# A hybrid decoder trunk with expert retrieval: GpSimd gathers the row of v ahead of the row of u in each slot

## The chip, the cores and the metric

The kernel runs on one core of a Trainium2 chip. The metric is the device time in microseconds, from one launch to its end. Three runs of the kernel before gave 3232.33, 3233.42 and 3233.64 us; the median is 3233.42 us. Lower is better.

## The reference

The reference is a decoder trunk of two layers on 512 tokens of width 1024, in float32. Each layer normalises x, runs three kinds of causal mixer side by side (a state-space group, a stick-breaking attention group and a sparse attention group), adds their projected output to x, and then adds a retrieval step:

```python
def peer_ffn(h, w_q, sub_keys, u_tab, v_tab):
    ...
        eidx = i1 * N_KEYS + i2
        g = jax.nn.softmax(cv, axis=-1)
        u = u_tab[eidx]
        v = v_tab[eidx]
        a = jax.nn.gelu(jnp.einsum('thkd,td->thk', u, xb).astype(jnp.float32), approximate=False)
        return jnp.einsum('thk,thkd->td', (g * a).astype(v.dtype), v)
```

For every token, 8 heads choose 16 experts each out of 16384. That is 128 experts per token, each with one row of 1024 numbers in the table u and one in the table v. The row of u is multiplied with the token (a dot product, then gelu and a gate weight), and the row of v is added to x with that weight. The change touches nothing but the order in which these rows are fetched.

## The kernel before, in words

The 512 tokens are four blocks of 128, one token to a partition. Two blocks make a step, so two layers make four steps (n = 0 to 3). A step has 256 **slots**: slot s stands for one expert of each of the 128 tokens of a block, 128 slots to a block, 16 to a head. In all there are 1024 slots (`GATHERS`), and each needs two gathers, one of u and one of v, of 128 rows of 4 KB (524,288 bytes).

All engines run one loop over s. The v side trails by `LAG` = 20 slots: in the pass for s the row of u belongs to slot s and the row of v to slot t = s - 20, since the weight of a head is known only when its 16 dot products are done. The last 20 passes have a v gather only.

- **GpSimd** (`pool_program`) issues both gathers, u at L1477 and v at L1490. The u rows land in a ring of 8 buffers, and so do the v rows. The gather of u for s waits until VectorE has used buffer s - 8 (`u_used`), at the start of a head also until the indices (`idx`) are there. The gather of v for t waits until t - 8 has been used: by TensorE (`v_used`) or by VectorE (`v_used_vector`). GpSimd takes its instructions in the order written, so a gather that waits holds all behind it.
- **VectorE** (`vector_program`) waits for u of slot s and forms the dot product (L1416). Where the slot t is its own (`BY_VECTOR`), it then waits for v of t and adds the weighted row to X (L1434). Every 16 slots it multiplies gelu and gate into the weights (L1424). At the end of a block it adds the sum that TensorE formed (L1439). Behind that come the pieces of the trunk and of the routing that are due at this slot.
- **TensorE** (`tensor_program`) takes the other slots: a matrix product of a diagonal of weights with the v rows, summed up in `acc` (L754). Before the first one of a block it waits for the sum of the block ahead (`x_done`). Then it does the trunk pieces due at this slot.
- **ScalarE** makes gelu (L1024) and the diagonals (L1032), and **SyncE** streams the weights of the trunk and writes the output.

VectorE takes one slot in 16 while no trunk work runs beside, otherwise every odd slot, and in the last step one in 4. The trunk of step n + 1 runs beside the gathers of step n, from its slot 90 on; the routing of a step (which finds the indices) runs into its own first 86 slots. In step 3 there is no trunk left to run beside.

Of the kernel before, what the change touches and what calls it, by code (L numbers as in the profile page):

```python
# [17 lines left out]
PEER_H, TOPK, KEYS = 8, 16, 128  # L18
# [18 lines left out]
PER_STEP = 2 * SLOTS  # L37
GATHERS = STEPS * PER_STEP
U_RING, V_RING, DIAG_RING = 8, 8, 5
# [182 lines left out]
def trunk(nc, x_dram, const_dram, param_dram, w_dram, u_dram, v_dram, out_dram):  # L222
# [4 lines left out]
    with ctx:  # L227
        def sb(name, shape, dt=fp32):
            return ctx.enter_context(nc.sbuf_tensor(name, shape, dt))
# [19 lines left out]
        u_rows, v_rows = sb("u_rows", [P, U_RING, D]), sb("v_rows", [P, V_RING, D])  # L249
        diag = sb("diag", [P, DIAG_RING, P])  # L250
        dots, gel, wgt = (sb(n, [P, 2, SLOTS]) for n in ("dots", "gel", "wgt"))
        idx = sb("idx", [P, 2, PER_STEP], u32)
# [77 lines left out]
        def sig(name):  # L330
            if name not in sems:
                sems[name] = ctx.enter_context(nc.semaphore(name))
            return sems[name]
# [36 lines left out]
        def nth(n, name, k):  # L370

            return n * PER[name] + k
# [54 lines left out]
        def before(v):  # L427

            return v - VECTOR_SUMS[v], VECTOR_SUMS[v]

        def phases_after(slot):

            return int((SLOT_OF <= slot).sum())
# [1009 lines left out]
        def pool_tracks(pool, n, chain):  # L1443
            l, p = divmod(n, PAIRS)
            heads = lambda t: t.rearrange("p (h d) -> p h d", d=HD)

            def all_():
                yield "n1b"
                if n == 0:
                    pool.wait_ge(sig("consts_in"), 16)  # L1450
                    made(G.memset(kcvcT[:], 0.0), "cache_zero")
                if p:
                    made(G.tensor_copy(xin[:, :, 0:TAPS - 1], tail[:]), "carry")
                else:
                    made(G.memset(xin[:, :, 0:TAPS - 1], 0.0), "carry")
                if p == 0:
                    yield "xt0"
                    wait_freed(pool, f"{n}.f7")
                    G.tensor_copy(tail[:], xin[:, :, PAIR:PAIR + TAPS - 1]).then_inc(sig("tail"), 1)
                    pool.wait_ge(sig("tail"), n // 2 + 1)  # L1460

            return [all_()]

        def pool_program(pool):
            chain = InOrder(pool, "pool_chain")
            run = Phases(lambda n: pool_tracks(pool, n, chain))
            run.upto(phases_after(-1))
            for s in range(GATHERS + LAG):
                n = s // PER_STEP
                if s < GATHERS:  # L1470
                    head = s % PER_STEP // TOPK
                    if s % TOPK == 0 and head <= PEER_H:
                        pool.wait_ge(sig("idx"), nth(n, "idx", 2 * head + 1 if head < PEER_H else 2 * PEER_H))
                    if s >= U_RING:
                        pool.wait_ge(sig("u_used"), s - U_RING + 1)
                    at_s = s % PER_STEP
                    pool.indirect_dma_start(  # L1477
                        out=u_rows[:, s % U_RING, :], out_offset=None, in_=u_dram,
                        in_offset=bass.IndirectOffsetOnAxis(ap=idx[:, n % 2, at_s:at_s + 1], axis=0),
                    ).then_inc(sig(f"u_in{s % U_RING}"), 16)  # L1480
                t = s - LAG
                if t >= 0:
                    if t >= V_RING:
                        old = t - V_RING
                        if BY_VECTOR[old]:
                            pool.wait_ge(sig("v_used_vector"), before(old)[1] + 1)
                        else:
                            pool.wait_ge(sig("v_used"), before(old)[0] + 1)
                    at_t = t % PER_STEP
                    pool.indirect_dma_start(  # L1490
                        out=v_rows[:, t % V_RING, :], out_offset=None, in_=v_dram,
                        in_offset=bass.IndirectOffsetOnAxis(ap=idx[:, t // PER_STEP % 2, at_t:at_t + 1], axis=0),
                    ).then_inc(sig(f"v_in{t % V_RING}"), 16)
                run.upto(phases_after(s - POOL_LAG))


# [29 lines left out]
        with nc.Block() as block:  # L1526
            @block.tensor
            def _(pe):
                tensor_program(pe)

            @block.scalar
            def _(act):
                scalar_program(act)

            @block.vector
            def _(dve):
                vector_program(dve)

            @block.gpsimd
            def _(pool):  # L1540
                pool_program(pool)

            @block.sync
            def _(sy):
                sync_program(sy)
# [18 lines left out]
```

## Time and profile before

| quantity | value |
|---|---|
| median of three runs | 3233.42 us |
| the profiled execution: its own time | 3229.1 us |
| its span | 3227.3 us |
| TensorE busy with matrix products | 2555.5 us (79%) |
| VectorE busy | 2429.2 us (75%) |
| GpSimd busy | 2115.9 us (66%) |
| ScalarE busy | 799.3 us (25%) |
| moved by the DMA engines | 1187.51 MB, mean 368 GB/s |
| of it by the gathers' queue | 1073.87 MB |

The profile comes from one execution, whose own time is 4.3 us under the median. The share of an engine is a mean over stretches that differ: in the first 300 us no gather can run yet, later the DMA engines, VectorE or TensorE set the pace in turn. In the rows of a timeline the first number is the start, the second the duration, and the brackets hold the idle time of the engine in front of the instruction and what ended it; "issue" means that it waited for nothing that the profile shows. The waits are given as engine and line, what was waited for, microseconds in total, times, longest.

### The profile page before, as it was taken

The page shows a single profiled execution, that of the slowest core. Times are in us where ns is not written, and L with a number is a line of the kernel's source. Part 1 is how long each engine was busy: PE and PEld are TensorE (multiplying, and loading weights), DVE is VectorE, ACT ScalarE, POOL GpSimd, SP SyncE. Part 2 cuts the span into 40 slices and gives each one's busy share as a digit, 9 for nine tenths or more (in the row PEclk, how much of TensorE's full clock was granted, in tenths as well). Part 3 has the DMA queues.
Part 4 walks back from the last instruction along what each step waited for, and adds up shares of the span by engine and source line. Part 5 has one row for each costly group of instructions (what it writes and reads, how often), then busy time and mean ns, then how long its engine had stood idle before and what let it go on. Part 6 is the DMA issues. An engine that isn't in the chain of part 4 may idle for free. (4 is left out here: it accounts for less than half of the span.)

```text
span 3227.3 us, 30187 instructions
## 1 busy us (share of the span) xinstructions
PE 2555.5 (79%) x8860; PEld 1512.6 (47%) x8860; DVE 2429.2 (75%) x5632; ACT 799.3 (25%) x1853; POOL 2115.9 (66%) x2059
## 2 busy tenths in 40 slices
PE   8877677898897686888788687899898587656667
PEld 7666433665464332665455342566566342222222
DVE  2324997768878997768878998758877999666664
ACT  2521222234321122223421122233431122111111
POOL 0001677657777777757776777766777777777775
PEclk9859799999898899898899799999899899998889
DMA  5104899999999999999999999999999999999999
GB/s 191 55 21 160 345 409 409 412 406 372 383 379 411 366 402 410 411 411 394 397 392 410 390 404 409 410 412 388 386 376 411 393 385 409 409 409 410 409 409 354
DMA packets 311313, 1187.51 MB, mean 368 GB/s; under 512 B 34544, under 2 KB 34544, under 8 KB 298352
## 3 DMA queue, kind: packets, MB, share of 16 engines
q0 software_dynamic: 294912, 1073.87, 84.7%
q1 hardware_dynamic: 16240, 111.72, 8.7%
q8 instruction: 73, 1.20, 0.1%
q14 instruction: 88, 0.72, 0.1%
HBM read 1183.36 MB, written 2.10 MB: 367 GB/s over the span
## 5 line engine op out<-in xcount | busy, mean ns | idle before, releaser
L754 PE MATMUL acc<-v_rows,diag 128*128 128x512 f32 x2728 | 1431.5, 659 | 485.7 <-DMA v_rows<-expert_v,idx 391.1
L1416 DVE CUSTOM_DVE_ANT_0 u_rows<-u_rows,h 128x1024 f32<-128x1024 f32 x1024 | 1231.4, 1216 | 398.4 <-DMA u_rows<-expert_u,idx 396.4
L1477 POOL DMA_INDIRECT u_rows<-expert_u,idx x1024 | 1057.0, 1032 | 625.6 <-DVE idx L1381 269.0
L1490 POOL DMA_INDIRECT v_rows<-expert_v,idx x1024 | 1057.2, 1032 | 425.6 <-issue 261.1
L754 PEld LDWEIGHTS acc<-v_rows,diag 128*128 128x128 f32 x2728 | 523.3, 207 | 1202.2 <-issue 985.4
L1434 DVE SCALAR_TENSOR_TENSOR X<-v_rows,wgt,X 128x1024 f32<-128x1024 f32 x342 | 439.2, 1284 | 43.5 <-DMA v_rows<-expert_v,idx 37.9
L1032 ACT ACTIVATE diag<-consts,wgt 128x128 f32<-128x128 f32 x682 | 255.1, 395 | 746.9 <-PE acc L754 567.9
L465 PE MATMUL bank<-HT,w_ring 128*128 128x256 f32 x1792 | 412.6, 386 | 2.2 <-DVE HT L1040 2.2
L465 PEld LDWEIGHTS bank<-HT,w_ring 128*128 128x128 f32 x1792 | 350.0, 196 | 93.3 <-issue 46.1
L474 PE MATMUL bank<-w_ring,HT 128*128 128x256 f32 (+1 forms) x1280 | 278.7, 375 | 2.6 <-ACT arena L765 2.6
L765 ACT ACTIVATE arena<-bank 128x256 f32<-128x256 f32 (+4 forms) x304 | 112.7, 382 | 664.5 <-PE bank L465 253.8
L474 PEld LDWEIGHTS bank<-w_ring,HT 128*128 128x128 f32 x1280 | 239.3, 193 | 56.3 <-issue 25.1
L1040 DVE TENSOR_TENSOR arena<-arena 128x256 f32<-128x256 f32 (+3 forms) x238 | 102.8, 435 | 4.7 <-ACT arena L765 3.5
L1024 ACT ACTIVATE gel<-dots 128x16 f32<-128x16 f32 x64 | 13.8, 216 | 332.1 <-DVE dots L1416 331.9
L686 PE MATMUL bank<-nkT,arena 64*128 64x128 f32 (+3 forms) x128 | 61.9, 571 | 29.9 <-ACT arena L961 27.2
L1416 DVE DVE_READ_ACCUMULATOR2_ANT dots<- 128x1 f32 x1024 | 85.0, 83 | 0.0
L734 PE MATMUL bank<-params,arena 128*128 128x128 f32 x256 | 43.0, 293 | 52.7 <-ACT arena L765 52.7
L456 PE MATMUL bank<-dg,X 128*128 128x128 f32 x256 | 42.9, 337 | 38.5 <-ACT dg L765 35.2
L1238 DVE TENSOR_REDUCE sm_mx<-bank 128x1 f32<-128x128 f32 (+3 forms) x64 | 31.3, 489 | 56.0 <-PE bank L687 56.0
L1290 DVE MAX8 arena<-arena 128x8 f32<-128x128 f32 (+1 forms) x192 | 52.9, 328 | 25.3 <-ACT arena L765 23.1
L734 PEld LDWEIGHTS bank<-params,arena 128*128 128x128 f32 x256 | 40.1, 203 | 63.3 <-ACT arena L765 56.8
L961 ACT ACTIVATE arena<-bank,sm_nm 128x128 f32<-128x128 f32 (+3 forms) x64 | 33.6, 526 | 128.7 <-DVE sm_nm L1239 50.0
(185 smaller groups left out, 1990.6 us busy)
## 6 DMA issues: line engine op xcount, KB each, us to landing
w_ring<-weights SPq DMA_DIRECT2D x100, 1024.0 KB, 8.0
u_rows<-expert_u,idx POOLq DMA_INDIRECT x1024, 11.0
v_rows<-expert_v,idx POOLq DMA_INDIRECT x1024, 11.2
X<-in_x SPq DMA_DIRECT2D x2, 1024.0 KB, 6.6
out<-X SPq DMA_DIRECT2D x4, 512.0 KB, 6.6
n2w_wide<-parameters SPq DMA_DIRECT2D x2, 512.0 KB, 8.4
params<-parameters SPq DMA_DIRECT2D x2, 412.0 KB, 7.6
consts<-constants SPq DMA_DIRECT2D x1, 749.5 KB, 6.4
```

What stands on the lines that cost most here:

```text
L465: last = T.matmul(out[:, 0:PAIR], cols(i)[:, k, m % 2 * P:(m % 2 + 1) * P], HT[:, k, :], start=(k == 0), stop=(k == KT - 1))
L474: last = T.matmul(out[:, 0:width], HT[:, k, blk[b]], cols(i)[:, k, 0:width], start=(k == 0), stop=(k == KT - 1))
L686: T.matmul(out[:, 0:width], nqT[base:base + 64, h // 2, blk[b]], nkT[base:base + 64, br, 0:width], start=True, stop=False)
L734: last = T.matmul(out[:, blk[b]], qT[m % 2][:, blk[b]], param("keys")[:, m % 2 * P:(m % 2 + 1) * P], start=True, stop=True)
L754: last = T.matmul(acc[:, at_h], diag[:, i % DIAG_RING], v_rows[:, t % V_RING, at_h], start=(at_t == 0), stop=(t == max(q for q in range(t ...
L765: return S.activation(dst, src, ACT.Copy, **k)
L1032: made(S.activation(diag[:, i % DIAG_RING], ident, ACT.Copy, scale=wgt[:, b % 2, at_t:at_t + 1]), "diag")
L1040: return V.tensor_tensor(out, in0, in1, op)
L1416: made(V.tensor_tensor_reduce(out=rows_u, in0=rows_u, in1=h2[:], scale=1.0, scalar=0.0, op0=ALU.mult, op1=ALU.add, accum_out=dots[:, b % 2 ...
L1434: made(V.scalar_tensor_tensor(Xb, v_rows[:, t % V_RING, :], wgt[:, b % 2, at_t:at_t + 1], Xb, ALU.mult, ALU.add), "v_used_vector")
L1477: pool.indirect_dma_start(out=u_rows[:, s % U_RING, :], out_offset=None, in_=u_dram, in_offset=bass.IndirectOffsetOnAxis(ap=idx[:, n % 2, ...
L1490: pool.indirect_dma_start(out=v_rows[:, t % V_RING, :], out_offset=None, in_=v_dram, in_offset=bass.IndirectOffsetOnAxis(ap=idx[:, t // PE ...
```

## The change

In the pass for s, GpSimd issued u of slot s and behind it v of slot s - 20. Now it issues v of slot s - 20 first, and u of slot s behind it. The waits stand with their gathers and move with them. The other engines' programs are as before.

```diff
--- before.py
+++ after.py
@@ -1467,17 +1467,6 @@
             run.upto(phases_after(-1))
             for s in range(GATHERS + LAG):
                 n = s // PER_STEP
-                if s < GATHERS:
-                    head = s % PER_STEP // TOPK
-                    if s % TOPK == 0 and head <= PEER_H:
-                        pool.wait_ge(sig("idx"), nth(n, "idx", 2 * head + 1 if head < PEER_H else 2 * PEER_H))
-                    if s >= U_RING:
-                        pool.wait_ge(sig("u_used"), s - U_RING + 1)
-                    at_s = s % PER_STEP
-                    pool.indirect_dma_start(
-                        out=u_rows[:, s % U_RING, :], out_offset=None, in_=u_dram,
-                        in_offset=bass.IndirectOffsetOnAxis(ap=idx[:, n % 2, at_s:at_s + 1], axis=0),
-                    ).then_inc(sig(f"u_in{s % U_RING}"), 16)
                 t = s - LAG
                 if t >= 0:
                     if t >= V_RING:
@@ -1491,6 +1480,17 @@
                         out=v_rows[:, t % V_RING, :], out_offset=None, in_=v_dram,
                         in_offset=bass.IndirectOffsetOnAxis(ap=idx[:, t // PER_STEP % 2, at_t:at_t + 1], axis=0),
                     ).then_inc(sig(f"v_in{t % V_RING}"), 16)
+                if s < GATHERS:
+                    head = s % PER_STEP // TOPK
+                    if s % TOPK == 0 and head <= PEER_H:
+                        pool.wait_ge(sig("idx"), nth(n, "idx", 2 * head + 1 if head < PEER_H else 2 * PEER_H))
+                    if s >= U_RING:
+                        pool.wait_ge(sig("u_used"), s - U_RING + 1)
+                    at_s = s % PER_STEP
+                    pool.indirect_dma_start(
+                        out=u_rows[:, s % U_RING, :], out_offset=None, in_=u_dram,
+                        in_offset=bass.IndirectOffsetOnAxis(ap=idx[:, n % 2, at_s:at_s + 1], axis=0),
+                    ).then_inc(sig(f"u_in{s % U_RING}"), 16)
                 run.upto(phases_after(s - POOL_LAG))
```

The line numbers move: the gather of v is L1479 in the changed kernel, that of u L1490.

On GpSimd, the place where the v gathers begin. Each row names line, target and source, and the semaphores waited for. Before:

```order
L1477 DMA u_rows<-expert_u,idx 128x1024 [waits u_used,idx]
L1477 DMA u_rows<-expert_u,idx 128x1024 [waits u_used] x4
L1490 DMA v_rows<-expert_v,idx 128x1024
L1477 DMA u_rows<-expert_u,idx 128x1024 [waits u_used]
L1490 DMA v_rows<-expert_v,idx 128x1024
L1477 DMA u_rows<-expert_u,idx 128x1024 [waits u_used]
```

And now:

```order
L1490 DMA u_rows<-expert_u,idx 128x1024 [waits u_used,idx]
L1490 DMA u_rows<-expert_u,idx 128x1024 [waits u_used] x3
L1479 DMA v_rows<-expert_v,idx 128x1024
L1490 DMA u_rows<-expert_u,idx 128x1024 [waits u_used]
L1479 DMA v_rows<-expert_v,idx 128x1024
L1490 DMA u_rows<-expert_u,idx 128x1024 [waits u_used]
```

The first v gather now stands ahead of u for slot 20 instead of behind it; from there on both orders alternate.

On GpSimd, the end of the program, from the last u gathers on. Before:

```order
L1477 DMA u_rows<-expert_u,idx 128x1024 [waits u_used]
L1490 DMA v_rows<-expert_v,idx 128x1024 [waits v_used]
L1477 DMA u_rows<-expert_u,idx 128x1024 [waits u_used]
L1490 DMA v_rows<-expert_v,idx 128x1024 [waits v_used_vector]
L1490 DMA v_rows<-expert_v,idx 128x1024 [waits v_used] x3
L1490 DMA v_rows<-expert_v,idx 128x1024 [waits v_used_vector]
```

And now:

```order
L1479 DMA v_rows<-expert_v,idx 128x1024 [waits v_used]
L1490 DMA u_rows<-expert_u,idx 128x1024 [waits u_used]
L1479 DMA v_rows<-expert_v,idx 128x1024 [waits v_used_vector]
L1490 DMA u_rows<-expert_u,idx 128x1024 [waits u_used]
L1479 DMA v_rows<-expert_v,idx 128x1024 [waits v_used] x3
L1479 DMA v_rows<-expert_v,idx 128x1024 [waits v_used_vector]
```

The last u gather (slot 1023) changed places with v of slot 1003, which waits for VectorE's use of slot 995. The v gathers from slot 1004 on are the same gathers at the same places of the sequence.

## Rows read from the trace of the kernel before

**Rows 1.** The page's slices: 40 equal parts, what the DMA engines moved in each, GB/s.

```profile
GB/s 191 55 21 160 345 409 409 412 406 372 383 379 411 366 402 410 411 411 394 397 392 410 390 404 409 410 412 388 386 376 411 393 385 409 409 409 410 409 409 354
```

**Rows 2.** Stretches: us; busy PE, PEld, DVE, ACT, POOL; clock, DMA share, GB/s.

```profile
720.00:960.00 240.00, 213.00 (x989) 138.43 (x988) 194.84 (x326) 92.16 (x203) 182.44 (x169) 0.93 0.99 377
1080.00:1140.00 60.00, 42.01 (x114) 22.82 (x114) 59.13 (x188) 10.34 (x26) 43.79 (x41) 0.83 0.95 345
1480.00:1660.00 180.00, 143.82 (x627) 85.45 (x626) 155.25 (x271) 64.94 (x169) 140.56 (x130) 0.89 1.00 388
1800.00:1860.00 60.00, 35.22 (x81) 16.48 (x80) 59.16 (x169) 8.98 (x24) 43.96 (x39) 0.74 0.99 376
2200.00:2400.00 200.00, 180.79 (x858) 114.16 (x858) 172.16 (x292) 83.90 (x188) 156.56 (x141) 0.93 0.99 378
2540.00:2620.00 80.00, 53.46 (x146) 28.25 (x146) 78.70 (x239) 15.60 (x38) 56.80 (x53) 0.85 0.98 368
2620.00:3180.00 560.00, 383.96 (x741) 144.68 (x739) 384.50 (x781) 78.59 (x206) 426.07 (x440) 0.91 1.03 409
```

**Rows 3.** The page's groups: line, operation, count | busy us, mean ns | idle before.

```profile
L1416 DVE CUSTOM_DVE_ANT_0 u_rows<-u_rows,h 128x1024 f32<-128x1024 f32 x1024 | 1231.4, 1216 | 398.4 <-DMA u_rows<-expert_u,idx 396.4
L1477 POOL DMA_INDIRECT u_rows<-expert_u,idx x1024 | 1057.0, 1032 | 625.6 <-DVE idx L1381 269.0
L1490 POOL DMA_INDIRECT v_rows<-expert_v,idx x1024 | 1057.2, 1032 | 425.6 <-issue 261.1
```

**Rows 4.** GpSimd's waits, whole run: total us, times, longest.

```profile
POOL v_rows L1490 <- PE acc L754: 158.3, 160, 5.4
POOL u_rows L1477 <- DVE dots L1416: 94.3, 161, 2.8
```

**Rows 5.** VectorE's waits for u: whole run, 720:960, 1480:1660, 2200:2400, in turn.

```profile
DVE u_rows L1416 <- DMA u_rows<-expert_u,idx: 396.4, 276, 6.3
...
DVE u_rows L1416 <- DMA u_rows<-expert_u,idx: 7.5, 6, 2.9
...
DVE u_rows L1416 <- DMA u_rows<-expert_u,idx: 3.7, 5, 1.3
...
DVE u_rows L1416 <- DMA u_rows<-expert_u,idx: 2.1, 2, 1.3
```

**Rows 6.** TensorE's waits: for v in 1480:1660, for the block's sum over the run.

```profile
PE acc L754 <- DMA v_rows<-expert_v,idx: 20.0, 13, 2.6
...
PE acc L754 <- DVE X L1439: 31.3, 4, 9.9
```

**Rows 7.** DMA issues in 2200:2400: count, median us from issue to landing.

```profile
v_rows<-expert_v,idx POOLq DMA_INDIRECT x71, 6.6
```

**Rows 8.** Timeline of GpSimd at 876 us: start, duration, what ended the idle time.

```profile
876.49 0.93 POOL L1477 DMA_INDIRECT u_rows<-expert_u,idx  x1 [0.31 <-issue]
...
880.10 0.94 POOL L1490 DMA_INDIRECT v_rows<-expert_v,idx  x1 [2.68 <-PE acc L754]
```

**Rows 9.** Timeline at 750 us: VectorE's weighted add, then GpSimd's issue.

```profile
750.42 1.28 DVE L1434 SCALAR_TENSOR_TENSOR X<-v_rows,wgt,X 128x1024 f32<-128x1024 f32 x1
...
750.54 1.97 POOL L1477 DMA_INDIRECT u_rows<-expert_u,idx  x1 [0.30 <-DVE dots L1416]
```

**Rows 10.** Timeline, first v gathers: issue of u for slot 20, dot of slot 20.

```profile
347.53 0.94 POOL L1477 DMA_INDIRECT u_rows<-expert_u,idx  x1 [0.30 <-issue]
...
357.17 1.21 DVE L1416 CUSTOM_DVE_ANT_0 u_rows<-u_rows,h 128x1024 f32<-128x1024 f32 x1
```

**Rows 11.** Timeline of the end, from the issue of v for slot 1004.

```profile
3181.19 0.94 POOL L1490 DMA_INDIRECT v_rows<-expert_v,idx  x1 [0.30 <-issue]
...
3194.25 1.22 DVE L1416 CUSTOM_DVE_ANT_0 u_rows<-u_rows,h 128x1024 f32<-128x1024 f32 x1 [1.33 <-DMA u_rows<-expert_u,idx]
...
3196.71 0.17 DVE L1424 TENSOR_TENSOR wgt<-gel,g 128x16 f32<-128x16 f32 x1
...
3196.91 25.99 PE L754 MATMUL acc<-v_rows,diag 128*128 128x512 f32 x60 [1.87 <-DMA v_rows<-expert_v,idx]
```

## The prediction

> **What bounds the kernel now.** I read the page's slices first, for the rate of the DMA engines. From the sixth slice on most values lie between 404 and 412 GB/s, and some between 366 and 397 [rows 1]. A gather is 524,288 bytes, so at 409 GB/s one takes 1.28 us and the pair of a slot 2.56 us. Then I cut the span into stretches [rows 2]. In 2620:3180, where no trunk work runs beside, the rate is 409 GB/s with the DMA engines always busy, while VectorE is busy 384.50 of 560 us and TensorE 383.96. There the transfers set the pace and every engine waits for rows. In six shorter stretches the rate is lower: 377, 345, 388, 376, 378 and 368 GB/s. Against 410 GB/s they lose (410 - rate) / 410 of their length: 19.3, 9.5, 9.7, 5.0, 15.6 and 8.2 us, together 67.3 us. All that the order of the gathers can win or lose in the middle of the program lies in these 820 us.
>
> Who sets the pace in them? In three of them (1080:1140, 1800:1860, 2540:2620) VectorE is busy 59.13 of 60, 59.16 of 60 and 78.70 of 80 us [rows 2]: it is the bound, and has no time in which to wait for a row. In the other three, TensorE and VectorE are both busy three quarters of the time or more, and the rest goes mostly to waits on each other. VectorE waits for u there only 7.5, 3.7 and 2.1 us, of 396.4 us over the whole run [rows 5]. TensorE waits for v 20.0 us in 1480:1660 [rows 6], the largest such sum in a stretch of this kind. So in the short stretches the rows are there before they are wanted. That is the second thing to read: the consumers' waits for rows lie nearly all where the DMA engines are full, and there a wait costs nothing that another order of the same bytes could give back.
>
> **What the change moves.** No gather, no byte and no wait is added or taken. In the middle of the program the sequence on GpSimd reads u, v, u, v in both kernels; what differs is which u stands beside which v. Each u now stands one place later against the v stream, and each v one place earlier against the u stream. One place is one issue on GpSimd (1032 ns on average and a gap of 0.30 us [rows 3, 9], so 1.33 us) or one transfer (1.28 us). I go through the places where this can matter.
>
> *The start of the v gathers.* u of slot 20 was issued at 347.53 us and its dot product began at 357.17 us [rows 10]. It now goes one issue later, at 348.8 us. A gather takes about 6.6 us to land where the queue is short [rows 7]; that gives 355.4 us, 1.8 us ahead of need. VectorE's routing is the cover. Term: 0; without the cover 1.3 us.
>
> *The stretches at 409 to 412 GB/s.* The same bytes pass in a full queue. VectorE gets u of its slot as the second row of the pair instead of the first, so its dot product starts 1.28 us later within the pair and the weighted add follows at once. One pair per 2.56 us still has to pass; dot product and add take 1.22 + 1.28 us [rows 3, 9], so it keeps up even where it has both. The v buffers that VectorE uses come free later after their landing, by 2.4 us: 1.28 us since v now lands a transfer before u, and some 1.1 us since the add ends later. A ring of 8 turns in 8 x 2.56 = 20.5 us, of which 6.6 us are needed for the landing. So 2.4 us more has room. Term: 0.
>
> *A stall on v.* GpSimd waited for TensorE's use of a v buffer 160 times, 158.3 us in all [rows 4]; without the usual 0.30 us gap in front of each issue that is 110 us of real stall. At 880.10 us it stood 2.68 us [rows 8]. The u gather of the same slot was issued before this stall (876.49 us) and now stands behind it. The v gather goes at the same time as before, for it is TensorE that frees it. The queue holds one gather less when the stall is over.
>
> *A stall on u.* It waited for a dot product 161 times, 94.3 us, 46 us of it real [rows 4]. Here the sign is opposite: the v gather in front of the wait is already out, so that the queue holds one gather more.
>
> The two meet in the short stretches, and count once each time that the DMA engines become the bound again: plus or minus 1.28 us per stretch, -7.7 to +7.7 us for the six. The stalls are equal in number, the longer ones are on v. I take 0 for the sum, since both kinds occur at the ends of these stretches, and keep both ends.
>
> *The wait for the block's sum.* TensorE waits for VectorE's add of the block's sum four times, 31.3 us [rows 6]. VectorE reaches that add after the dot product of the same slot, which can be one transfer later: 4 x 1.28 = 5.1 us at most. Where the DMA engines are full the queue covers it, and in the VectorE-bound stretches u is there long before. Term: 0, upper end 5.1 us.
>
> *The end.* TensorE's last work is a run of 60 products from 3196.91 us that takes 25.99 us. It starts as v of slot 1004 lands, which was issued at 3181.19 us [rows 11]. That gather keeps its place in the sequence. u of slot 1023 lands 1.28 us later: its dot product moves from 3194.25 to 3195.5 us, and the last weights from 3196.71 to about 3198.1 us. They are wanted first for slot 1008, after three slots of 25.99 / 15 = 1.73 us, at 3202.1 us. The three slots hide the delay with 4 us to spare. Term: 0.
>
> **Sum.** 0 on the profiled execution's 3229.1 us. Its own time is 4.3 us under the median of the runs, so the forecast for the median is 3233 us.
>
> *GpSimd's issues beside VectorE's adds.* An issue takes 0.93 or 0.94 us when nothing is in its way [rows 8]. The one at 750.54 us was released by a dot product, began 0.12 us after a weighted add (750.42 us, 1.28 us long) and took 1.97 us [rows 9]: it ended 0.81 us after the add, as if it had begun only when the add was over. The average of all u gathers is 1032 ns, and that of all v gathers too [rows 3], so (1.032 - 0.94) x 1024 = 94 us of such delay lie on each kind. The Trainium skill, "SBUF — State Buffer", section "Who interferes with whom", says that a VectorE instruction with two inputs in SBUF contends with a GpSimd instruction that reads SBUF. By that rule the new order would help, for the gather behind a dot product met the add that follows it, and now a v gather stands in front. The trace agrees with the rule on the single row, but by the equal averages neither kind suffers more than the other.
>
> **The rivals.**
>
> *Faster: fewer of these collisions.* For it: the row at 750.54 us, and 161 u gathers released by a dot product. Against: GpSimd's speed must bind, and it binds only where the consumers wait for rows. In the six stretches VectorE waits for u 7.5 + 3.7 + 2.1 = 13.3 us. If all of that went: 3233 - 13 = 3220 us. More likely half, 3226 us.
>
> *Slower: the v ring as a gate for u.* Place: the short stretches with TensorE behind, as at 880 us. Now a stall on v also stops the next u, and VectorE, where it has used up its lead, waits for it. Price: 1.28 us for each of the six stretches, and the 5.1 us of the block's sum, if the v stall is the last in each and the cover is thin: 3233 + 7.7 + 5.1 = 3246 us; the first part alone gives 3241 us. It decides if TensorE's stalls are those that end the short stretches, and if a u gather behind one lands later than 8 slots of lead allow. For it: 110 us of real stall on v against 46 on u. Against: VectorE is busy throughout in three of the stretches and has a lead of up to 8 rows.
>
> *The change does next to nothing in itself.* That is my forecast: the interleaved stream is the same but for its two ends, and both are covered.
>
> **How the numbers follow.** Runs of this kernel differ by 1.3 us among themselves; 0.2%, or 6.5 us, is about what a measurement can tell from no change. I give the forecast (3227 to 3239 us) 0.66. Slower, by the v ring as gate or by a shift of the trunk's work that I have not seen, 0.19, at 3240 to 3246 us. Faster, by the collisions or by TensorE's earlier v rows, 0.15, at 3220 to 3226 us. The range from 3224 to 3242 us leaves out less than 2 in 10, and holds the ends of -7.7 and +7.7 us nearly whole.
>
> **What would show it.** Right: the same stretches at 409 GB/s, the short ones at about 377, 345, 388, 376, 378 and 368; the sum of VectorE's waits for u near 396 us, though the waits for v at its weighted add vanish, as v lands first. GpSimd's stalls move between the lines: the ones on v grow, since it asks for them one issue earlier, and those on u shrink. The end still starts with the landing of v for slot 1004 and runs 26 us. The collision rival would show as an average issue clearly under 1032 ns together with a higher rate in the short stretches. The slower rival would show as VectorE's waits for u in the short stretches well over 13.3 us, and a rate below 377 GB/s in 720:960. The forecast is wrong if a short stretch gets longer by more than two gathers (2.6 us), or if the end starts with something else than v of slot 1004.

## The result: slower by 0.3%, and the profile after

The changed kernel takes 3241.49 us (median of 12 runs, 3236.62 to 3245.04), the kernel before on the same chip 3231.74 us (12 runs, 3226.21 to 3233.94). The ratio is 1.003, with a 95% interval from 1.0021 to 1.0039: slower, by about 10 us. The time lies in the predicted range, at its upper end, but that is luck: the forecast was no change, and the change found is clear of the scatter. The profiled execution took 3241.40 us, its span is 3239.6 us; before it was 3229.1 us, so the two traces differ by 12.3 us.

The slices of the page after the change, which answer to [rows 1]:

```profile
GB/s 190 53 15 164 345 409 409 411 398 376 379 382 411 351 404 410 410 412 396 395 395 410 388 389 409 410 412 379 393 369 411 397 372 409 409 409 410 409 409 354
```

The plateau still stands at 409 to 412. The 14th slice fell from 366 to 351, the 24th from 404 to 389 and the 33rd from 385 to 372; each of these holds the way out of one of the three stretches in which VectorE computes the routing. A slice is a fortieth of the span, and the two spans differ, so a slice after lies a few us later than the one before. The 28th to 30th, in trunk work, go down and up (388, 386, 376 to 379, 393, 369). The stretches of [rows 2] in the kernel after (same columns):

```profile
720.00:960.00 240.00, 210.26 (x974) 136.39 (x973) 193.53 (x324) 92.49 (x203) 178.55 (x166) 0.93 0.99 378
1080.00:1140.00 60.00, 38.64 (x98) 19.98 (x99) 58.90 (x178) 11.46 (x30) 35.87 (x39) 0.77 0.93 327
1480.00:1660.00 180.00, 142.46 (x630) 85.55 (x631) 156.97 (x274) 67.39 (x172) 140.65 (x130) 0.90 1.01 389
1800.00:1860.00 60.00, 34.40 (x85) 18.87 (x83) 59.14 (x172) 10.65 (x26) 37.79 (x40) 0.74 1.00 381
2200.00:2400.00 200.00, 178.59 (x858) 110.64 (x859) 172.45 (x293) 87.53 (x197) 151.76 (x139) 0.94 0.99 376
2540.00:2620.00 80.00, 50.17 (x134) 27.85 (x135) 78.88 (x235) 13.23 (x33) 49.80 (x51) 0.82 0.98 367
2620.00:3180.00 560.00, 397.43 (x759) 154.16 (x757) 383.24 (x805) 79.70 (x211) 425.09 (x441) 0.88 1.03 408
```

The three stretches with trunk work (first, third, fifth) move at the old rate within 2 GB/s. Of the three with VectorE as the bound only 1080:1140 shows a loss, 327 for 345 GB/s. These cuts are too narrow: what is lost there is lost at their edges. So I cut the same places wider, with both flanks. Before:

```profile
980.00:1200.00 220.00, 167.31 (x468) 89.66 (x466) 212.95 (x665) 41.56 (x103) 159.45 (x152) 0.88 1.00 391
1740.00:1950.00 210.00, 151.91 (x407) 76.60 (x406) 206.99 (x652) 40.76 (x99) 151.87 (x145) 0.89 1.02 400
2490.00:2800.00 310.00, 223.52 (x549) 101.71 (x547) 281.64 (x826) 57.62 (x140) 229.50 (x225) 0.92 1.01 399
```

After:

```profile
980.00:1200.00 220.00, 164.48 (x480) 90.06 (x479) 212.42 (x663) 40.70 (x102) 149.82 (x152) 0.89 1.00 386
1740.00:1950.00 210.00, 156.40 (x408) 81.83 (x407) 203.91 (x639) 39.94 (x98) 138.82 (x143) 0.85 1.01 393
2490.00:2800.00 310.00, 224.98 (x552) 104.98 (x551) 282.00 (x840) 56.58 (x138) 219.24 (x226) 0.91 1.01 396
```

A stretch loses (rate before - rate after) x length / 410: 2.7, 3.6 and 2.3 us, together 8.5 us. The same sum over 320:650, 650:980, 1200:1740, 1950:2490 and 2800:3180 gives 1.6 us, and the other 2.2 us of the 12.3 lie before 320 us, where no v gather has been issued, or in the rounding. So the loss has a place: the routing stretches with their flanks. Below, "the routing loss" is this sum of three, against the first profile of before. One GB/s of rounding is 0.5 to 0.8 us in it.

The groups of [rows 3] after:

```profile
L1416 DVE CUSTOM_DVE_ANT_0 u_rows<-u_rows,h 128x1024 f32<-128x1024 f32 x1024 | 1232.6, 1216 | 470.5 <-DMA u_rows<-expert_u,idx 460.1
L1490 POOL DMA_INDIRECT u_rows<-expert_u,idx x1024 | 1038.6, 1014 | 592.9 <-DVE idx L1381 270.8
L1479 POOL DMA_INDIRECT v_rows<-expert_v,idx x1024 | 1028.8, 1005 | 516.7 <-issue 247.8
```

An issue takes 1014 or 1005 ns instead of 1032. That is 47 us less work on GpSimd, and the kernel is slower all the same. What grew is waits (total us, times, longest; whole run), for [rows 4], [rows 5] and one line that had no match there:

```profile
DVE u_rows L1416 <- DMA u_rows<-expert_u,idx: 460.1, 337, 6.3
...
POOL v_rows L1479 <- PE acc L754: 147.3, 131, 6.5
POOL v_rows L1479 <- DVE X L1434: 117.2, 75, 4.6
...
POOL u_rows L1490 <- DVE dots L1416: 60.1, 160, 2.7
```

The second line of GpSimd is new in size: the v gather waits 75 times, 117.2 us, for VectorE's weighted add. The same wait before:

```profile
POOL v_rows L1490 <- DVE X L1434: 5.6, 7, 1.3
```

Of the 117.2 us, 20.6, 25.2 and 19.4 us lie in the three wide stretches, and only 1.3 us in 2620:3180, where the transfers set the pace throughout. GpSimd's waits for a dot product fell in the wide stretches from 17.5 + 18.1 + 17.1 = 52.7 to 7.1 + 5.8 + 7.3 = 20.2 us. Those on TensorE went from 20.9 to 26.0.

How the wait arises is seen in the timeline at the first routing stretch (start, duration, ..., idle time and what ended it). Before, a VectorE slot with an add, and GpSimd's pair:

```profile
1014.74 1.22 DVE L1416 CUSTOM_DVE_ANT_0 u_rows<-u_rows,h 128x1024 f32<-128x1024 f32 x1
...
1015.88 1.28 DVE L1434 SCALAR_TENSOR_TENSOR X<-v_rows,wgt,X 128x1024 f32<-128x1024 f32 x1
1016.23 1.74 POOL L1477 DMA_INDIRECT u_rows<-expert_u,idx  x1 [1.27 <-DVE dots L1416]
1018.28 0.93 POOL L1490 DMA_INDIRECT v_rows<-expert_v,idx  x1 [0.30 <-issue]
```

After, such a slot again:

```profile
1019.00 1.21 DVE L1416 CUSTOM_DVE_ANT_0 u_rows<-u_rows,h 128x1024 f32<-128x1024 f32 x1
...
1020.13 1.28 DVE L1434 SCALAR_TENSOR_TENSOR X<-v_rows,wgt,X 128x1024 f32<-128x1024 f32 x1
1021.68 0.94 POOL L1479 DMA_INDIRECT v_rows<-expert_v,idx  x1 [2.75 <-DVE X L1434]
1022.92 0.94 POOL L1490 DMA_INDIRECT u_rows<-expert_u,idx  x1 [0.30 <-issue]
```

Both gathers of a pass stand on buffers that VectorE used 8 slots ago, and in VectorE's program the dot product comes first and the add behind it. Before, GpSimd asked in the same order, u and then v. Now it asks for v first, waits for the add, and u, whose buffer has been free for the length of the add, waits behind it. The u issue started 0.27 us after the dot product's end before, and 2.7 us after it now.

Part of this is paid back. Before, the u issue ran beside the add and took 1.74 us instead of 0.94, and ended 0.81 us after the add; now the v issue is undisturbed and ends 1.21 us after it. So the first and the second gather of such a pair each end 0.4 us later than before. But the two have changed places: u now ends 2.45 us after the add instead of 0.81, so 1.6 us later, and v 1.21 instead of 2.05, so 0.8 us sooner. In the 60 passes from 20 ahead of each step's first slot (256, 512, 768), the time from the end of u's issue to its dot product fell from 19.5, 19.6 and 19.1 us to 17.6, 18.2 and 17.3 us (means, from the two traces), by 1.9, 1.4 and 1.8. An exchange of places alone would take one issue, 1.24 us. For the v rows of the same numbers that VectorE adds, the time from the end of the issue to the add grew from 18.8, 18.8 and 18.9 us to 20.1, 20.3 and 20.4.

Where VectorE falls behind, slot by slot (start of a slot's dot product after, less that before, in us). The second row is the same from a second profile of each kernel, before_again and after_again below:

| slot | 200 | 220 | 256 | 320 | 456 | 496 | 552 | 588 | 712 | 756 | 820 | 848 |
|---|---|---|---|---|---|---|---|---|---|---|---|---|
| first pair | 1.5 | 6.2 | 4.2 | 4.4 | 5.0 | 6.9 | 6.8 | 10.8 | 9.9 | 10.6 | 10.4 | 13.7 |
| second pair | -0.2 | 4.2 | 2.7 | 2.1 | 5.0 | 1.2 | 1.1 | 4.3 | 4.1 | 6.7 | 6.8 | 9.8 |

From 256 to 320, 496 to 552 and 756 to 820 VectorE stays as late as it was, within 0.6 us. These slots hold the stretches in which it is the bound. It falls behind on the way out in both pairs (552 to 588: 4.0 and 3.2 us, 820 to 848: 3.3 and 3.0). On the way in it does so at slots 200 to 256 (2.7 and 2.9 us), while 456 to 496 differs in sign between the pairs (1.9 and -3.8) and 712 to 756 in size (0.7 and 2.6). The two profiles of before differ by up to 2.1 us in these slots, so a single value of 1 or 2 us says nothing. 1.28 us of any value belongs to u as the second row of the pair where transfers set the pace.

The end, for [rows 11], after:

```profile
3192.58 0.94 POOL L1479 DMA_INDIRECT v_rows<-expert_v,idx  x1 [0.30 <-issue]
...
3207.87 1.22 DVE L1416 CUSTOM_DVE_ANT_0 u_rows<-u_rows,h 128x1024 f32<-128x1024 f32 x1 [1.33 <-DMA u_rows<-expert_u,idx]
...
3209.25 25.99 PE L754 MATMUL acc<-v_rows,diag 128*128 128x512 f32 x60 [3.15 <-DMA v_rows<-expert_v,idx]
3210.22 0.17 DVE L1424 TENSOR_TENSOR wgt<-gel,g 128x16 f32<-128x16 f32 x1
```

It starts with v of slot 1004 and takes 25.99 us, as before; the last weights come 0.97 us after its start, and the first three slots cover that. The last run of products starts 12.34 us later than before and the dot product of slot 1023 13.62 us later: 1.28 us more, as predicted, and covered.

### The profile page after: what moved, and what is told of

Its sections match the earlier page's. It is cut to its first block and busy times, and to the rows that moved or that the text cites. A ratio compares the mean times of both kernels' runs of the same rounds, so it can differ in the third digit from the quotient of the medians.

```text
span 3239.6 us, 30187 instructions
## 1 busy us (share of the span) xinstructions
PE 2554.6 (79%) x8860; PEld 1516.5 (47%) x8860; DVE 2422.4 (75%) x5632; ACT 797.2 (25%) x1853; POOL 2069.2 (64%) x2059
## 5 line engine op out<-in xcount | busy, mean ns | idle before, releaser
L1416 DVE CUSTOM_DVE_ANT_0 u_rows<-u_rows,h 128x1024 f32<-128x1024 f32 x1024 | 1232.6, 1216 | 470.5 <-DMA u_rows<-expert_u,idx 460.1
L1490 POOL DMA_INDIRECT u_rows<-expert_u,idx x1024 | 1038.6, 1014 | 592.9 <-DVE idx L1381 270.8
L1479 POOL DMA_INDIRECT v_rows<-expert_v,idx x1024 | 1028.8, 1005 | 516.7 <-issue 247.8
L1434 DVE SCALAR_TENSOR_TENSOR X<-v_rows,wgt,X 128x1024 f32<-128x1024 f32 x342 | 438.4, 1282 | 17.8 <-DMA v_rows<-expert_v,idx 17.8
L456 PEld LDWEIGHTS bank<-dg,X 128*128 128x128 f32 x256 | 42.4, 254 | 63.9 <-issue 51.5
```

What stands on the lines that cost most here:

```text
L456: last = T.matmul(out[:, blk[i]], src[:, k * P:(k + 1) * P], dg[:, at_d + b], start=True, stop=True)
L1416: made(V.tensor_tensor_reduce(out=rows_u, in0=rows_u, in1=h2[:], scale=1.0, scalar=0.0, op0=ALU.mult, op1=ALU.add, accum_out=dots[:, b % 2 ...
L1434: made(V.scalar_tensor_tensor(Xb, v_rows[:, t % V_RING, :], wgt[:, b % 2, at_t:at_t + 1], Xb, ALU.mult, ALU.add), "v_used_vector")
L1479: pool.indirect_dma_start(out=v_rows[:, t % V_RING, :], out_offset=None, in_=v_dram, in_offset=bass.IndirectOffsetOnAxis(ap=idx[:, t // PE ...
L1490: pool.indirect_dma_start(out=u_rows[:, s % U_RING, :], out_offset=None, in_=u_dram, in_offset=bass.IndirectOffsetOnAxis(ap=idx[:, n % 2, ...
```

## The experiments

Theory after the result: the v gather now waits for the add behind the dot product and holds u back ("the v ring as a gate"). Rivals: an effect of the landing order at the consumers (v lands before u, while VectorE uses u first); TensorE's stalls on v alone; chance between executions. Differences in us below are (ratio - 1) x 3230 us. All edits are against the kernel before unless said otherwise; in their diffs `gather_u(s)` and `gather_v(t)` stand for its two blocks of L1470 to L1494, each with its waits.

**v_earlier: v one slot further ahead (more of the suspected wait).**

```
-            for s in range(GATHERS + LAG):      # u of s, then v of s - LAG
+            for s in range(GATHERS + LAG - 1):
+                if s >= LAG - 1:
+                    gather_v(s - LAG + 1)
                 if s < GATHERS:
+                    gather_u(s)
```

> GpSimd issues v of slot s-19 ahead of u of slot s: a whole slot more for v on top of the change (each u stands two places later against the v stream than before, instead of one). Handover theory: each time the DMA engines hand the pace to VectorE, its row of u is late by one transfer per place (1.28 us), and each time TensorE's v buffer ends a stall, one u gather per place is still unissued; 2 x 1.28 us for each of the three routing stretches and place, and about 0.8 us for each trunk stretch and place. The change cost 10 us by its profile, so two places should cost about 20 us: ratio to the kernel before 1.005 to 1.007, with steps of about 5 us in the bytes moved at 1100, 1850 and 2600 us. Rival, the new wait of v gathers for VectorE's add as such (117 us against 5.6): it is there once, about 1.003, or somewhat more in every stretch alike. Rival, chance in how issues meet VectorE's instructions: anything between 0.998 and 1.005, no steps of one size.

Measured: 3261.81 us, ratio 1.0099 (1.0083 to 1.0115), +32 us. Its two waits on v:

```profile
POOL v_rows L1488 <- DVE X L1434: 161.7, 83, 7.0
POOL v_rows L1488 <- PE acc L754: 137.7, 121, 9.3
```

The wait on the add grows from 5.6 over 117.2 to 161.7 us and the time by 0, 10 and 32 us. The direction is that of the theory, the size more than the 1.005 to 1.007 expected. The routing loss is 19.1 us, and here the other stretches lose 12.4 us too.

**u_ahead: u one slot further ahead (less of it).**

```
+            gather_u(0)
             for s in range(GATHERS + LAG):
+                if s + 1 < GATHERS:
+                    gather_u(s + 1)
+                if s >= LAG:
+                    gather_v(s - LAG)
```

> The other way: GpSimd issues u of slot s+1 ahead of v of slot s-20, so that each u stands one place earlier against v than in the kernel before. Handover theory: the three routing stretches give 2 x 1.28 us each back, 7.7 us in all, unless TensorE, whose v rows now land a transfer later, loses it again: 0.9975 to 1.000. Rival, the wait for the add: it was 5.6 us already in the kernel before, nothing to gain, 1.000. Rival, chance: no steps.

Measured: 3236.32 us, 1.0024 (1.0014 to 1.0033). A miss: it isn't faster than before but slower. Its waits show another gate:

```profile
DVE X L1434 <- DMA v_rows<-expert_v,idx: 318.9, 136, 4.9
...
POOL u_rows L1475 <- DVE dots L1416: 170.1, 215, 5.1
```

u now waits for the dot product of the slot after the one whose add v waits for, and v stands behind that wait. VectorE waits 318.9 us for v at its add, before it was 37.9. So a cost arises on this side too, and its waits look the same with the roles exchanged: the gather that asks too early gates the other. No run shows that this wait is the cause of the 8 us that u_ahead costs.

**add_first: the change, and VectorE does the add ahead of the dot product.** GpSimd's order is that of the changed kernel, and the add that frees v's buffer comes first in VectorE's slot.

```
 in vector_program, for each slot s:
+                t = s - LAG
+                if t >= 0 and BY_VECTOR[t]:
+                    (the waits and the scalar_tensor_tensor of L1428 to L1435)
                 if s < GATHERS: ... dot product of s ...
-                if t >= 0 and BY_VECTOR[t]: ...
```

> The change (v first) and in the same pass VectorE does its weighted add of v ahead of its dot product of u, so that it takes the rows in the order in which they land. Handover theory: the entry's part goes (VectorE has its pair done 1.2 us after the second landing, as before), the exit's stays: 3 to 5 us over the kernel before, 1.001 to 1.0015; the v gathers' wait for the add falls from 117 us to under 60 us. If the entry isn't part of the price: 1.003 as in the change.

Measured: 3233.09 us, 1.0006 (0.9997 to 1.0015). Its waits on v:

```profile
POOL v_rows L1482 <- PE acc L754: 189.5, 171, 5.8
...
POOL v_rows L1482 <- DVE X L1409: 28.4, 19, 3.4
```

The wait on the add falls from 117.2 to 28.4 us, and the time by most of the 10 us, though v still lands before u. That speaks against TensorE's stalls, for GpSimd's waits on them are longer here (189.5 us) than after (147.3). It doesn't separate the wait from the landing order, since VectorE now also uses the rows in the order in which they land. The next pair of runs bears on that. In the trace of add_first the slots of the way out still lose 3.8 and 2.4 us (552 to 588, 820 to 848, against the first profile of before), which fits the expectation that the exit's part stays, though the median shows no price that can be told from none. The routing loss of its profile is 3.6 us.

**v9_u7_vfirst and v9_u7_ufirst: both orders with a v ring of 9 and a u ring of 7.** With 9 the v gather waits for the add of one slot earlier, and with 7 the u gather for the dot product of one slot later, so v's buffer can't be the later of the two to come free.

```
-U_RING, V_RING, DIAG_RING = 8, 8, 5
+U_RING, V_RING, DIAG_RING = 7, 9, 5
```

> The change with 9 buffers for v and 7 for u. If the v ring is the gate that holds u back at the exits, one more v buffer takes away that part: against the same rings with u first (next kernel) 0 to 4 us, and it may beat the change itself. If it is not, the difference between the two orders stays at 10 us.

> The kernel before with 9 buffers for v and 7 for u, the control of the last one. With the v ring as the gate (158 us of waits on it against 94 us on u) this order gains a little from the ninth buffer: 0.998 to 1.000. If the u ring is as tight: 1.000 to 1.004.

Measured: v first 3235.35 us, 1.0014 (1.0006 to 1.0023); u first 3238.11 us, 1.0023 (1.0014 to 1.0032). With these rings the changed order is no slower than the old, where 0 to 4 us was expected with the v ring as the gate and 10 us without; the medians lie 2.8 us the other way. The wait on the add is gone with v first:

```profile
POOL u_rows L1490 <- DVE dots L1416: 194.9, 237, 2.9
...
POOL v_rows L1479 <- DVE X L1434: 5.5, 2, 3.2
```

Here v lands before u and VectorE uses u first, as in the change, and the wait on the add is gone. All that is left over the kernel before is 4.5 us (1.9 to 7.4), and the shorter u ring is in it. Unless the ninth v buffer gains something elsewhere (with u first it didn't, 1.0023), the landing order is at most a part of the 10 us, and the price isn't one of the order in itself; it hangs on which gather's buffer comes free last. The two rings changed together, so what each of them does isn't known; a v ring of 9 beside a u ring of 8 was not tried. v first with these rings is still slower than the kernel before, so they are no way to use the change.

**v_first_near and v_first_far: where the change costs.** The new order in passes 252 to 291 around each step's boundary (where VectorE is the bound), or everywhere else.

```
+                v_first = s >= PER_STEP - 4 and (s + 4) % PER_STEP < 40      # near
+                v_first = s < PER_STEP - 4 or (s + 4) % PER_STEP >= 40       # far
+                if v_first and s >= LAG: gather_v(s - LAG)
                 if s < GATHERS: gather_u(s)
+                if not v_first and s >= LAG: gather_v(s - LAG)
```

> v first only in the passes 252 to 291 of each 256 (from 4 slots ahead of a step to its slot 35), that is in the stretch in which VectorE is the bound and where TensorE's stall ends it; u first elsewhere. Handover theory: only the exit's part of the price, 1.28 us for each of three stretches, 3.8 us: ratio 1.001. Wait-for-the-add rival: some of the 117 us lies here, but the DMA engines are not the bound; 1.000. Chance: any.

> v first everywhere but in the passes 252 to 291 of each 256. Handover theory: the entry's part (1.28 us for each of three stretches, 3.8 us) and what the trunk stretches cost (2.5 us) stay, the exit's part goes: about 6 us over the kernel before, ratio 1.002. Wait-for-the-add rival: nearly all of the change's price stays, 1.003.

Measured: near 3235.53 us, 1.0018 (1.0009 to 1.0027), +5.8; far 3237.66 us, 1.0022 (1.0013 to 1.0031), +7.1. Their waits on the add are 67.5 and 65.0 us. The two parts together give 12.9 us for the whole's 9.7. Each interval is nearly 3 us wide to either side, so this fits a cost that adds up over places, and doesn't prove one. Both parts cost something, also the 40 passes in 256, where 1.000 or 1.001 was expected. Each of them also switches between the orders, with two gathers of v or two of u in a row at every switch, which the change doesn't have; how much of their price that is was not tested.

**exit_only and entry_only: the two sides of such a stretch.** The same code with `v_first` in passes 24 to 35 of a step, or in 216 to 255 and 0 to 7.

```
+                v_first = s >= PER_STEP and 24 <= s % PER_STEP < 36          # exit
+                v_first = s >= 216 and (s + 40) % PER_STEP < 48              # entry
```

> v first only in passes 24 to 35 of each step but the first, where TensorE's stall ends the stretch in which VectorE is the bound. Handover theory: the exit's transfer alone, 1.28 us for each of three routing stretches, 3.8 us in the staircase of moved bytes there and nothing in the trunk stretches: ratio 1.001. If instead the price builds up through the whole VectorE-bound stretch by the waits for its add, most of it is missing here: 1.000.

> v first only in passes 216 to 255 of a step and 0 to 7 of the next, where the DMA engines hand the pace to VectorE; u first elsewhere, also where TensorE's stall ends the stretch. Handover theory: the entry's part, 3 x 1.28 = 3.8 us in the routing stretches (the exit alone showed 3.9 us in its profile), nothing lasting in the trunk stretches: 1.0005 to 1.0015. If the price sits at the exits alone: 1.000.

Measured: exit 3232.34 us, 1.0005 (0.9996 to 1.0015), no difference that can be told; entry 3236.87 us, 1.0022 (1.0013 to 1.0031), +7.1 us, more than expected. The routing loss is 3.4 us in both profiles, each taken in an execution some 3.5 us over its median. GpSimd's waits for the add are 5.9 us in exit_only, as before the change (5.6): from pass 20 of a step on VectorE takes one v slot in 16 only, so passes 24 to 35 hold nearly none of the suspected waits. And VectorE falls behind at slots 552 to 588 and 820 to 848, after pass 35 of the step. So exit_only tested neither, and what the way out costs isn't settled by it. entry_only has 36.8 us of these waits and costs 7.1 us, so having v first on the way in, switches included, is enough for a price. In its trace VectorE loses 1.3, 2.9 and 1.9 us on the three ways in (slots 200 to 256, 456 to 496, 712 to 756; against before_again 1.3, 0.9 and 2.4) and 0.1 and 1.2 us on the ways out (against before_again -0.8 and 0.3), where the change loses 4.0 and 3.3.

**u_first_add_first: the old order, with the add ahead of the dot product.** If order of use and order of asking must agree, this mismatch should cost too.

```
 vector_program as in add_first; GpSimd's program as before
```

> GpSimd as before (u first), but VectorE does its add of v ahead of the dot product of u: the fourth corner of the square of GpSimd's order and VectorE's. If what counts is that rows are fetched in the order in which VectorE uses them, this corner is as bad as the change or worse, since the dot product now waits for the second row and for the add: 1.003 to 1.008. If v first on GpSimd is bad by itself: 1.000.

Measured: 3232.43 us, 1.0012 (1.0003 to 1.0021). A miss: much less than expected. The mismatch shows in the waits, but not in the time:

```profile
DVE X L1409 <- DMA v_rows<-expert_v,idx: 355.5, 157, 4.9
...
POOL u_rows L1480 <- DVE dots L1426: 150.9, 236, 3.1
```

Here v waits behind u for a dot product though its own buffer was freed an add earlier, and that costs 4 us (1.0 to 6.8) where the change costs 10. Against add_first (1.0006), which has the same VectorE program and differs in GpSimd's order alone, it is 2 us, less than these intervals can tell. In the 60 passes around each step's first slot, u keeps its time from issue to dot product here (19.5, 19.7 and 19.3 us, before 19.5, 19.6 and 19.1), and the v rows that VectorE adds lose 1.2 to 1.5 us of theirs; in the change it is u that loses. That u's delay is the dear one is a guess from this, which no run tests; why the one mismatch is so much cheaper stays open.

**before_again and after_again: both kernels unchanged, for the scatter between profiles.**

```
 (no edit)
```

> The kernel before, profiled a second time, to see how far the staircase of moved bytes differs between two executions of one kernel. Every other profile lost about 3.5 us against the first one in the trunk stretch at 2180 to 2500 us, kernels without any change there too; expected is the same 3 us here, and less than 1.5 us in the routing stretches.

> The change, profiled a second time. Handover theory: about 8 us in the three routing stretches again (2.7 us each); the trunk stretches may come out otherwise.

Measured: 3230.81 us, 1.0005 (0.9995 to 1.0015), and 3240.86 us, 1.0038 (1.0023 to 1.0053). The 3 us expected in the trunk stretch at 2180 to 2500 us did not come in before_again: 390 GB/s in both profiles of before. The rates in the three wide stretches and the loss by them, for every run:

| kernel | GB/s | routing loss | other stretches | ratio |
|---|---|---|---|---|
| before | 391, 400, 399 | 0 | 0 | |
| before_again | 391, 399, 398 | 1.3 | 1.3 | 1.0005 |
| after | 386, 393, 396 | 8.5 | 1.6 | 1.0030 |
| after_again | 385, 392, 394 | 11.1 | -0.5 | 1.0038 |
| v_earlier | 380, 389, 389 | 19.1 | 12.4 | 1.0099 |
| u_ahead | 390, 395, 397 | 4.6 | -0.3 | 1.0024 |
| v_first_near | 389, 397, 396 | 4.9 | 2.6 | 1.0018 |
| v_first_far | 390, 396, 397 | 4.1 | 0.5 | 1.0022 |
| entry_only | 389, 397, 398 | 3.4 | 3.7 | 1.0022 |
| exit_only | 389, 397, 398 | 3.4 | 2.6 | 1.0005 |
| add_first | 389, 395, 399 | 3.6 | 2.9 | 1.0006 |
| u_first_add_first | 390, 396, 398 | 3.3 | 4.0 | 1.0012 |
| v9_u7_vfirst | 389, 394, 398 | 4.9 | 1.3 | 1.0014 |
| v9_u7_ufirst | 390, 394, 398 | 4.4 | -1.1 | 1.0023 |

The loss in the routing stretches comes back in the second profile of after and not in that of before. The nine edited kernels between 1.0005 and 1.0024 all show 3.3 to 4.9 us of it, whatever their time: the profiled executions lie up to 6 us off their medians, and the rounding is 0.5 to 0.8 us for each GB/s. So this column tells after and v_earlier from the rest, and ranks nothing among the others. The other stretches swing by some 4 us among kernels, so no cause is read from them. The kernel before stays the fastest.

## Why the prediction was wrong

*What bounds the kernel.* Right: the plateau kept its rate within 1 GB/s, and the loss lies outside it, most of it about the stretches at lower rates.

*The start and the end.* Right, both cost nothing: the dot product of slot 20 is 1.7 us later, and that of slot 0, ahead of all v gathers, is 1.6 us later already; the end begins with v of slot 1004 and takes 25.99 us. The row at 357.17 us in [rows 10] is misread, though: it is the dot product of slot 18. Slot 20's began at 362.21 us, so the cover was 6.8 us and not 1.8, and the term of 0 is safer than the prediction says.

*"The stretches at 409 to 412 GB/s ... Term: 0."* The term is right: 2800:3180 moves at 409 GB/s in both kernels, with 1.3 us of waits on the add. This step saw that the v buffers of VectorE come free later, but weighed that against the ring in the full queue alone. There it took 6.6 us for the landing, which is the value of 2200:2400; in 2800:3180 the median was 13.1 us before. 2.4 us more had room even so. It carried the later release no further, into the stretches where VectorE or TensorE sets the pace.

*"A stall on v" and "a stall on u": "I take 0 for the sum."* This is the step that failed. Its list held GpSimd's waits for TensorE and for the dot product, as equal kinds of opposite sign. The wait that the change makes isn't in it: v in front of its pass waits for VectorE's add, which stands behind the dot product, and u is held behind v. It was 5.6 us before, and the sum has no term for it. It became 117.2 us, while GpSimd's waits on TensorE went from 158.3 to 147.3 us only. In place of the 0 the runs showed about 10 us, of which 8.5 to 11.1 us of transfer time lie in the three routing stretches with their flanks. add_first and the ring of 9 take the wait away, and most of the price goes with it (1.9 and 4.5 us are left); v_earlier lengthens it, and the price grows to 32 us. The upper end of +7.7 us was near the measured 10 us, but by luck: it counts one transfer for each of six stretches, and the loss came in three, by another wait.

*The faster rival.* Its premise held: the issues became shorter, 1032 to 1014 and 1005 ns, as the rule of the Trainium skill ("SBUF — State Buffer", section "Who interferes with whom") would have it. It was worth nothing, as its own objection said, for GpSimd's speed doesn't bind. In the pair shown above the collision was a wait in another form: 0.8 us of the add's time, taken by an issue that had already begun.

*The slower rival.* "The v ring as a gate for u" at 3241 us is half of the mechanism that came, v's wait holding u back, and its size. It had another release in mind: TensorE's, in the stretches with trunk work, which move at the old rate. So that its figure fits is luck, as above; and it got 0.19 for its chance. The argument against it, that VectorE is busy throughout and has a lead of 8 rows, misled the forecast. VectorE isn't slowed while it is the bound (slots 496 to 552 and 756 to 820), but it falls behind after that. A reading that fits, and that no run isolates: rows that are not fetched in that time are missing when the transfers are the bound again.

*What would show it.* Of the forecast's signs, VectorE's waits for u didn't stay near 396 us (460.1), and its waits for v fell from 37.9 to 17.8 us and didn't vanish. GpSimd's stalls moved as said, up on v (by the add alone) and down on u, from 94.3 to 60.1 us. The forecast's own limit, a stretch longer by more than 2.6 us, was passed in one of the three wide stretches clearly (3.6 us) and reached in another (2.7). The slower rival's signs came in part: waits for u in 720:960, 1480:1660 and 2200:2400 rose from 7.5 + 3.7 + 2.1 = 13.3 to 19.9 + 11.9 + 4.0 = 35.8 us, while the rate in 720:960 stayed at 378.

**What stays open.** How the 8.5 to 11.1 us divide over the single waits, and between way in and way out; how much of the 10 us, if any, is the landing order; why u_ahead costs as much as it does and u_first_add_first so little; what a switch of order costs by itself; and the price of a u ring of 7.

## What to carry to other kernels

When one in-order queue issues gathers for two ring buffers, begin with asking in the order in which the consumer frees them: the gather in front holds back all behind it, and a wait on the later release takes the earlier one along. How much a mismatch costs has to be measured; here it was 10 and 32 us with v asked too early, and 4 to 8 us where u was. To price a change of order, list for each gather which instruction frees its buffer and what stands ahead of that in the consumer's program, even where the wait is a few us in the trace of before. And look at the places where the bound passes from one engine to another; a stretch with a full queue, or with a full engine, says nothing about them.

## What the runs showed of the hardware

A gather's issue on GpSimd takes 0.94 us, and 1.74 us where it began 0.35 us after the start of VectorE's add of 1.28 us. It ended 0.81 us after the add both here and at 750 us [rows 9], where it began 0.12 us after the start and took 1.97 us. Both rows look as if the issue did its work only once the add was over. In the new order GpSimd is busy 47 us less with its issues (two profiles of before differ by 7 us), and that saved no time of the kernel.
